# Laying out the experts of a mixture-of-experts stage by turns of their groups

## The reference, cut to what matters

```python
grp = argmax(h @ rg_w + rg_b)                    # one of 4 groups
in_group = (h @ re_w + re_b).reshape(T, 4, 8)[arange(T), grp]
top_val, top_idx = lax.top_k(in_group, 2)        # two of the group's 8 experts
gate = p_grp * softmax(top_val)
out[t] = sum over both: gate * ((silu(h @ w_gate[e]) * (h @ w_up[e])) @ w_down[e])
```

## Time and profile before

| | us |
|---|---|
| median of 3 runs | 2141.33 |
| lowest, highest | 2134.90, 2147.95 |
| the profiled execution | 2141.47 |
| its span | 2140.2 |
| TensorE busy | 1894.2 (89%) |
| DMA, mean over the span | 171 GB/s |
| the block loop on TensorE, first `gate_up` to last `down` | 1536.2 to 2103.5 |

### The profile page before, as it was taken

The page is one execution under the profiler, slowest core; times in us unless marked ns, Lnnn a source line. Parts: engine busy times, 40 slices in busy tenths (PEclk is TensorE's granted clock), DMA queues, the critical chain, the costliest instruction groups (busy, mean ns, idle before and its releaser), DMA issues.

```text
span 2140.2 us, 24139 instructions
## 1 busy us (share of the span) xinstructions
PE 1894.2 (89%) x8578; PEld 1300.5 (61%) x8578; DVE 836.5 (39%) x1154; ACT 409.3 (19%) x740; POOL 969.3 (45%) x492
## 2 busy tenths in 40 slices
PE   5999999899998999999998899966696877789992
PEld 4888888787775778888886666645432323233330
DVE  5444443310444675444434898763310000001013
ACT  3111100100443421111001435413010000001111
POOL 5888877677443687888875333212010000001001
PEclk9999999999999999999999999978698998889996
DMA  3333382333111232333332121102999999998973
GB/s 131 93 94 98 109 330 91 130 97 92 56 50 40 74 93 89 98 98 98 102 98 78 59 67 62 50 26 77 379 383 399 396 397 396 394 400 293 381 309 132
DMA packets 60161, 365.89 MB, mean 171 GB/s; under 512 B 7184, under 2 KB 7568, under 8 KB 47696
## 3 DMA queue, kind: packets, MB, share of 16 engines
q1 hardware_dynamic: 45648, 323.51, 42.2%
q10 hardware_dynamic: 10192, 27.32, 3.4%
q0 software_dynamic: 4272, 14.42, 2.1%
HBM read 384.36 MB, written 27.00 MB: 192 GB/s over the span
## 4 chain that ended last, share of the span: by engine, by line
PE 69%; DMA 14%; DVE 11%; ACT 3%; issue 1%; POOL 1%; SPq 0%; DVEq 0%; ACTq 0%; POOLq 0%
PE bank L448 29%; DMA big<-w_up_in 13%; PE bank L419 11%; PE bank L1683 9%; PE bank L680 4%; PE bank L1236 3%; PE bank L1698 3%; DVE big L1013 3%; PE bank L467 2%; PE bank L1344 2%; PE bank L598 1%; DVE state L998 1%; PE bank L658 1%; ACT work L614 1%; PE bank L1624 1%
## 5 line engine op out<-in xcount | busy, mean ns | idle before, releaser
L265 POOL TENSOR_TENSOR weights_hi_parts<-ring,ones 128x1024 fp32r<-128x1024 f32 (+1 forms) x176 | 356.3, 2024 | 306.8 <-PE bank L448 137.5
L267 POOL TENSOR_TENSOR ring_parts<-ring,weights_hi_parts 128x1024 fp32r<-128x1024 f32 (+1 forms) x176 | 473.8, 2692 | 13.8
L448 PE MATMUL bank<-attention_buffers_parts,weights_hi_parts 128*128 128x512 f32 x832 | 328.1, 394 | 29.2 <-POOL ring_parts L267 17.7
L1683 PE MATMUL bank<-big,work 128*64 128x512 f32 x1040 | 304.2, 642 | 48.4 <-DMA big<-w_up_in 48.2
L448 PE MATMUL bank<-state_parts,weights_hi_parts 128*128 128x512 f32 x832 | 325.6, 391 | 0.0
L448 PE MATMUL bank<-attention_buffers_parts,ring_parts 128*128 128x512 f32 x832 | 325.6, 391 | 0.0
L1768 POOL TENSOR_TENSOR small<-small 128x1 f32<-128x1 f32 x36 | 6.9, 193 | 476.3 <-DVE small L1629 476.3
L419 PE MATMUL bank<-big_parts,weights_hi_parts 128*128 128x512 f32 x704 | 217.1, 389 | 1.2 <-POOL ring_parts L267 1.2
L1683 PEld LDWEIGHTS bank<-big,work 128*64 128x64 f32 x1040 | 102.7, 148 | 160.0 <-issue 157.2
L448 PEld LDWEIGHTS bank<-attention_buffers_parts,weights_hi_parts 128*128 128x128 f32 x832 | 157.4, 189 | 65.5 <-POOL ring_parts L267 17.7
L852 POOL TENSOR_TENSOR ring_parts<-ring,weights_hi_parts 128x1024 fp32r<-128x1024 f32 x32 | 81.0, 2533 | 234.4 <-ACT weights_hi_parts L849 234.4
(11 more groups left out here) (347 smaller groups left out, 2681.1 us busy)
## 6 DMA issues: line engine op xcount, KB each, us to landing
ring<-wdense_in SPq DMA_DIRECT2D x176, 512.0 KB, 3.6
big<-w_up_in SPq DMA_DIRECT2D x39, 2048.0 KB, 33.1
state<-w_down_in SPq DMA_DIRECT2D x27, 2048.0 KB, 42.2
big<-w_gate_in SPq DMA_DIRECT2D x26, 2048.0 KB, 26.7
ring<-w_gate_in SPq DMA_DIRECT2D x13, 2048.0 KB
attention_buffers<-w_down_in SPq DMA_DIRECT2D x13, 2048.0 KB
ring<-wff_in SPq DMA_DIRECT2D x32, 704.0 KB, 4.1
y_rows<-big ACTq DMA_DIRECT2D x1, 12288.0 KB, 42.1
```

The source lines that it names most:

```text
L265: po.tensor_tensor(hi, raw, ones[:, 0:1].to_broadcast([128, words]), ALU.mult).then_inc(PO.sem, 1)
L267: po.tensor_tensor(lo, raw, hi.bitcast(F32), ALU.subtract) \
L448: m = pe.matmul(out, x, y_, start=j + n == 0, stop=j == len(pairs) - 1 and n == len(ts) - 1)
L1683: m = pe.matmul(first_products[b][m_ * BS:(m_ + 1) * BS, :], xet[:, k * BS:(k + 1) * BS], sets[b][m_][:, k * D_EXP:(k + 1) * D_EXP], start ...
```

## The change

The expert list is reordered: index i of the new list is expert (i mod 4) * 8 + i // 4, so the list reads 0, 8, 16, 24, 1, 9, 17, 25, 2, ... The expert weights, the columns of the router's expert matrix and its biases are put into that order on the host. On the chip only the mask of line 1491 changes: the experts of a group are now 4 apart, so the mask is added through a four-dimensional view. All index arithmetic on the chip stays, and now numbers the experts in the new order. Every engine has the same instructions in the same order as before: 2414 rows on PE, 804 on DVE, 504 on ACT, 297 on POOL and 174 on SP in the built program, the conditional loads among the last. What differs is the data that steers them.

```diff
-    E3 = lg_e.rearrange("p (g e) -> p g e", e=PER_GRP)
-    DV.run(dv.tensor_tensor(E3, E3, over_last(gmask, NT * N_GRP, PER_GRP), ALU.add))
+    E4 = lg_e.rearrange("p (t e g) -> p t e g", t=NT, g=N_GRP)
+    DV.run(dv.tensor_tensor(E4, E4, gmask3.unsqueeze(2).to_broadcast([128, NT, PER_GRP, N_GRP]), ALU.add))
...
-    row[ROWS["b_route"] + 8:ROWS["b_route"] + 40] = one["router_expert_b_2"]
+    by_turns = np.arange(N_EXP).reshape(N_GRP, PER_GRP).T.reshape(-1)
+    row[ROWS["b_route"] + 8:ROWS["b_route"] + 40] = one["router_expert_b_2"][by_turns]
...
-    wr = chunks(np.concatenate([one["router_group_w_2"], one["router_expert_w_2"]], 1))
+    wr = chunks(np.concatenate([one["router_group_w_2"], one["router_expert_w_2"][:, by_turns]], 1))
...
     def expert(w):
+        w = w[by_turns]
         e, k, n = w.shape
```

## The result

The changed kernel takes 2107.65 us (median of 4 runs, 2104.03 to 2113.00), against 2142.14 for the kernel before. The ratio is 0.984, with a 95% interval of 0.982 to 0.987, and the medians lie 34.5 us apart. The profiled execution took 2113.0 us with a span of 2111.7.

What follows compares the result with a forecast made beforehand. Two regimes bound the loop: weight transfers in loading slots (17.16 us), TensorE in the late stretch (11.83). Spared load 14.6, idle DMA 7 and end 8 sum to 29.6 us, from 2141.5 to 2112; range 2098 to 2131.

Steps and rivals of the forecast that it cites:

- The counts and the lists: Expert token counts give 37 blocks, 13 turns, 32 loads before and 31 after, with eight slots without a load listed.
- The spared load: Block loop's weight transfers: three tiles less to move, 14.6 us; rival that only this counts, 2127 us, chance 0.06.
- The idle engines: DMA engines running dry in slots 24 to 29 before, not after: gain 7 us, at most 10.
- The end: Last slots: TensorE no longer behind, last `gate_up` ending 9 to 11 us after the last tile, not 18.4; gain 8.
- The sum: Whole kernel: 14.6 + 7 + 8 = 29.6 us off 2141.5, giving 2112 us.
- slot-by-slot check: Hand count of the block loop: last `gate_up` ends at 2089 to 2091 before, 2061 to 2065 after; 28 to 32 earlier.
- The mask: Router's group mask on VectorE, 0.30 us: a tenth less to 0.3 more through the new view, taken as 0.
- The waits of `gate_up` for weights: TensorE's waits in the block loop: some 50 us after the change in place of 74.
- TensorE's clock: Rival: `gate_up` in slots 13 to 24 costs 1.6 us more each; 2121 us, chance 0.07.
- The result store: Rival: ScalarE's copies wait for result stores and set the loop's pace; at 15.5 us each 2163 us, chance 0.04.
- formula (1558 + 36 P): Last `gate_up`'s end if each result copy took P us: at 14.8 no gain (2139), deciding from 15.2.

Runs made afterwards that it cites:

- 32 to 31 loads: Another order by turns with 32 loads and spread skips, against the kernel before: 2126.9 us, ratio 0.993; compared with the changed kernel, which has 31 loads.
- 31 to 30: Changed kernel (31 loads) with groups ordered 0, 1, 3, 2, giving 30 loads: 2100.2 us, then 2096.7 beside the change's 2111.1 on one chip.
- filled heads: Changed kernel with groups ordered 0, 1, 3, 2, so chain 2 starts with expert 24, which has tokens, not empty 16; 30 loads: 2100.2, then 2096.7 us.
- second execution of the change: Profiled execution from the changed kernel's unaltered rerun on one chip with the version of 30 loads; that rerun measured 2111.1 us, ratio 0.984 to the kernel before.
- nothing to skip: Every slot from 3 on loads its set (39 loads): 2214.9 us as an edit of the kernel before, 2217.2 us as an edit of the changed kernel.

## Why the prediction was right, point by point

It forecast 2112 us. The median is 2107.65, and the profiled execution, against whose like the sum was made, took 2113.0. The mechanism held: each of its three terms is seen in the trace. That the sum came within 1 us of one pair of profiled executions is in part luck, since the medians lie 34.5 us apart where it said 29.6.

**The counts and the lists** held in each of the eight skips and in the 6.3 MB. This step carries all the others.

**The spared load**, 14.6 us. Between two spread orders it comes to 16 or 19 us (32 to 31 loads: 2126.9 against 2107.65 and 2111.1) on different chips, and to 14.4 (31 to 30) on one, though only to 7.5 in the runs before those. These differences hold the idle times of the orders too, so they bear the price out no closer than by some 5 us.

**The idle engines**, 7 us of at most 10. The last tile landed near 2054, where the prediction's last paragraph said 2053, and at 2074.8 before: 21 us earlier. The first packet of the weights came 1.9 us later, though (1499.3 against 1497.4), so from the first to the last it is 22.4 us less, of which 14.6 are the load and 8 this term. The trace shows it directly: the share of 0.75 from 1930 to 1970, some 10 us, is gone. The 10 that the prediction counted as idle were right, and 7 was a little low.

**The end**, 8 us. From the last tile to the end of the last `gate_up` it was 18.4 us before and is 9 now: 9.4 gained. The working had 9 to 11. Slot 37's tiles landed at 2043.7, some 10 us before the last, and the `gate_up` after that wait took 7.09 us and not 8.6.

**The sum** of the three is 29.6 us, and 30.4 were measured at the end of the last `gate_up`, or 32 counted from the first packet of the weights. What follows it took 48.9 us and not 47. The slot-by-slot check was as close: slot 12 at 1700 where it began at 1704, slot 25 at 1856 where it began at 1860, the end at 2061 to 2065 where it came at 2062.8. Slots 27 to 31 took 17.2 each, from 1890.5 to 1959.3. But its "28 to 32 earlier" sets its own end after against the chip's before. Against its own 2089 to 2091 before, it is 24 to 30. The mask takes 293 ns where it took 294. The waits of `gate_up` for weights fell from 74.4 us to

```profile
PE bank L1683 <- DMA big<-w_up_in: 49.6, 17, 7.5
```

where some 50 were said.

**TensorE's clock** cost nothing that shows in the loop. `gate_up` stayed at 7.02 us throughout slots 13 to 25, and where it was longer, after waits, the DMA share was 1.01 all the same.

**The result store** came nearer than the prediction's words made it sound. ScalarE waited for it 24 times instead of 14, and in the middle stretch at each copy but the first:

```profile
ACT ring L1723 <- DMA y_rows<-ring: 126.7, 24, 6.9
```

The copies there, in order of time:

```profile
1717.20 0.60 ACT L1723 ACTIVATE ring<-bank 128x512 f32<-128x512 f32 x1 [3.71 <-PE bank L1698]
1729.56 0.60 ACT L1723 ACTIVATE ring<-bank 128x512 f32<-128x512 f32 x1 [4.24 <-DMA y_rows<-ring]
1742.06 0.60 ACT L1723 ACTIVATE ring<-bank 128x512 f32<-128x512 f32 x1 [4.91 <-DMA y_rows<-ring]
...
1884.58 0.60 ACT L1723 ACTIVATE ring<-bank 128x512 f32<-128x512 f32 x1 [5.51 <-DMA y_rows<-ring]
```

Fourteen intervals take 167.4 us, 11.96 each against TensorE's 11.83. The longest are 12.4 and 12.5. The drift reached some 2 us of the 5 that are free, and the next `down` never waited for it. The price at which the kernel would have become slower, 15.2 us, was far off. By the prediction's own formula (1558 + 36 P) a pace of 14.1 would already have passed the forecast's end, and that was far off too. Where the prediction says 11.9 us "in every saturated stretch", show it in one, from 1992 to 2063, beside the single 14.20.

What the prediction didn't foresee is that a different layout of the same idea would do better. It noted that expert 16 is loaded for nothing, at 14.6 us, and left it there.

## What to carry to other kernels

Where a loop takes work from two sides, one limited by transfers and one by an engine, in blocks that differ in which side they load, the order of the blocks decides how much of the two overlaps. Spread the blocks that need no transfer so that the little that the buffers can queue (here 20 to 34 us by the prediction's reckoning, and with filled heads three skips among five slots already left the engines idle for 3 us) bridges each run of them, and let none of them pile up at the end. Before looking for a new layout, write the list of blocks out from the data, with a load or a skip at each, and sum both sides over each stretch. Here that gave the time within 0.3%, and the same count put the better order at 2093, where 2097 to 2100 were measured. Such an order is tuned to its inputs: another seed of tokens has other counts.

## What the runs showed of the hardware that wasn't expected

**A late start of TensorE is mostly hidden in a loop that the transfers pace, but not wholly.** In the second execution of the change the router's last products ran at 1.2 GHz throughout (granted clock 0.50). The first of these rows is of the change's second profiled execution, the second of the kernel before (start us, length us):

```profile
1503.49 6.69 PE bank L448 x32
```
```profile
1499.72 3.51 PE bank L448 x32
```

The first `gate_up` began at 1543.1 and not at 1539.0 as in the change's first execution, 4 us later, and the last one ended at 2063.0 against 2062.8. But this execution had reached its router 2.2 us earlier, and by the DMA engines' records the weights began at 1497.1 and not at 1499.3. So TensorE was some 6 us late, and from the first packet to the end of the last `gate_up` it took 2.4 us longer. SP issues the first load of slot 3 only at the end of slot 0's `gate_up` (at 1552.0, against 1549.0), and meanwhile the engines ran dry. In the first execution the share was 1.00 from 1545 to 1565, and here it was 0.77:

```profile
1545.00:1565.00 20.00, 19.68 (x102) 7.54 (x98) 1.91 (x5) 3.14 (x5) 2.19 (x4) 0.97 0.77 256
```

**A small store behind full engines takes four times as long.** A result's 128 KB lands 2.3 us after the issue when the engines are free, and after 8.2 to 11.2 us, 9.5 in the middle, when they are full of 2 MB loads (the change, 1700 to 1850). It stays about that long when every slot loads and none is skipped (the new order with nothing to skip, 1600 to 1900: 7.8 to 11.0, 9.6 in the middle).

**The profile's line on HBM doesn't tell what was moved.** It gives the same MB before and after, although the queue moved 6.3 MB less (here after):

```profile
HBM read 384.36 MB, written 27.00 MB: 195 GB/s over the span
```

The same MB stand in the pages of all the runs, with 39 loads (367.55 MB on SP's queue) and with the three of slots 0 to 2 alone (141.05 MB). So a skipped transfer seems to be counted as if it had been carried out. The MB of the queues tell what was moved.
